# Product-key expert retrieval for 8 samples, laid out by (head, sample) instead of by sample

## The chip, the cores and the metric

The kernel runs on one core of one Trainium2 chip. The metric is the device time of one execution in microseconds; the runs are summed up by their median.

## What is computed

One inference step of a decoder layer for a prompt of 256 tokens and for 8 samples of one token each, D = 2048, all in float32. The change touches the last sublayer, the experts (PEER):

```python
def one(xb):
    q = (xb @ w_pq).reshape(PEER_BLOCK, PEER_HEADS, 2, half)          # 8 heads, 2 x 128
    s1 = jnp.einsum('thd,kd->thk', q[:, :, 0], k1).astype(F32)        # 128 keys
    s2 = jnp.einsum('thd,kd->thk', q[:, :, 1], k2).astype(F32)
    t1, i1 = lax.top_k(s1, PEER_TOPK)                                 # 16 of 128
    t2, i2 = lax.top_k(s2, PEER_TOPK)
    cand = (t1[..., :, None] + t2[..., None, :]).reshape(...)         # 256 candidates
    cidx = (i1[..., :, None] * PEER_KEYS + i2[..., None, :]).reshape(...)
    top, pos = lax.top_k(cand, PEER_TOPK)
    eidx = jnp.take_along_axis(cidx, pos, axis=-1)
    g = jax.nn.softmax(top, axis=-1)
    u = u_tab[eidx]
    v = v_tab[eidx]
    a = jax.nn.gelu(jnp.einsum('thkd,td->thk', u, xb).astype(F32))
    return jnp.einsum('thk,thkd->td', (g * a).astype(v.dtype), v)
```

So each token has 8 heads, each head picks 16 of 16384 experts, and each expert is one row of 2048 numbers (8 KB) in `peer_u` and one in `peer_v`.

## The kernel before

**Blocks.** The 264 tokens are three blocks, `BLOCKS = (P, P, TS)`: two of 128 prompt tokens, one token on a partition, and one of the 8 samples. A token has `SLOTS` = 128 experts (8 heads x 16). Block 0 and block 1 gather their rows slot by slot: one indirect DMA fetches one row of 8 KB for each of 128 partitions. For the samples the 8 x 128 experts are spread over all 128 partitions, so that 8 gathers of u and 8 of v do for all of them; before, partition 16 t + k holds slot k of every head of sample t.

**Order of the expert stage.** The stage runs from about 1340 us to the end. POOL issues all gathers in one order, `pool_gathers` (L1874): first block 0's u rows; then pairs (`pairs`, L1898), of block 1's u row and block 0's v row; then the samples' u and v rows, beside block 1's v rows; then the rest of block 1's v rows. There are 8 slots of 128 x 2048 numbers: 4 for u (even) and 4 for v (odd). Before a u gather POOL waits for a count of dots (`peer_used`), before a v gather for a count of weighted rows (`v_used`). A new index group is copied by two small POOL copies for every four pairs (`indices`, L1892).

**VectorE** forms the dot of each u row with the token's vector (`dve_paired_dots`, L1972, instruction at L1978). Between dots it does the retrieval. For blocks 0 and 1 that goes in 4 parts of 2 heads each; the samples are a part by themselves, number `LAST` = 8, with all 8 heads. A part has three steps, set between loops of dots by hand in the vector program:

```python
            dve_paired_dots(dve, 18, 20)
            dve_keys(dve, LAST)
            dve_paired_dots(dve, 20, 23)
            dve_candidates(dve, LAST)
            dve_paired_dots(dve, 23, 25)
            dve_experts(dve, LAST)
            dve_weights(dve, 1)
            dve_weights(dve, 2)
            dve_paired_dots(dve, 25, 28)
            dve_samples_experts(dve)
```

One loop turn is 4 dots, so `(20, 23)` is 12 dots. A part of block 1 has 8 dots between its steps, and 8 more before the next part's keys. `dve_keys` (L1727) takes the best 16 of 128 scores for each head and key half, `dve_candidates` (L1738) sums them to 256 candidates a head and takes the best 16 of them, both by `dve_sixteen` (L1704: MAX8 at L1715 and L1722, MATCH_REPLACE8 at L1718, FIND_INDEX8 at L1719 and L1725). `dve_experts` (L1758) turns the positions into expert numbers, with six wide operations (L1781, L1784, L1786, twice each). The weights are a softmax: `act_softmax` (L1686) on ScalarE, `dve_weights` (L1794) on VectorE. All operations of VectorE work on rows of a partition, so the samples' ones run on 8 partitions, with 8 heads side by side.

**TensorE** forms the weighted sum of v rows as products with a diagonal matrix of weights (`pe_weighted`, L2004, instruction at L2010); the diagonals come from ScalarE (L1996). The samples' scores are made before the sums begin (`pe_keys(pe, 2)`, L1692, copied out by `act_keys`, L1698). After 26 turns of block 0's sums `pe_samples_experts` (L1826) spreads the samples' expert numbers and weights over the 128 partitions with a selector matrix (`sel`), and `dve_samples_experts` (L1834) masks and reduces them to 8 columns. `sel` also spreads the samples' vectors (`pe_samples_expand`, L1813), and `selT` gathers the partial sums at the end (`pe_samples_sums`, L2066).

Of the kernel before, what the change touches and what calls it, by code (L numbers as in the profile page):

```python
# [23 lines left out]
P = 128  # L24
# [26 lines left out]
for _name, _n in (("ident", P), ("ones", P), ("d0", P), ("d1", TP), ("cb", QB * TP), ("mc", QB * 16), ("ds", PAST + 1),  # L51
                  ("dcs", NC), ("t", TP), ("sel", P), ("selT", TS), ("kmask", 16), ("selk", P), ("kvm", KV), ("iota", 16), ("column", 63), ("pidx", 1),
                  ("half_pi", 1), ("eps", 1)):
    C[_name] = (sum(n for _, n in C.values()), _n)
# [4 lines left out]
def constants():  # L59
    c = np.zeros((P, NCONST), np.float32)  # L60

    def put(name, value):
        a, n = C[name]
        c[: value.shape[0], a:a + n] = value
# [20 lines left out]
    put("sel", (p[None] // 16 == np.arange(TS)[:, None]))  # L85
    put("selT", (p[:, None] // 16 == np.arange(TS)[None]))
    put("kmask", (p[:, None] % 16 == np.arange(16)[None]))
    put("selk", (p[None] % 16 == n[:, None]))
# [41 lines left out]
def build(nc, A):  # L130
    with ExitStack() as ctx:
# [1422 lines left out]

        BLOCKS = (P, P, TS)
        HN = [mv_n[:, 0:D], mv_n[:, D:2 * D], b_st[:, :]]
        XN = [y_t[:, 0:D], y_t[:, D:2 * D], c_st[:, :]]
# [18 lines left out]
        LAST = 2 * PARTS  # L1576
        RETRIEVAL.append((2, 0, PH, LAST * marks(2)[2], x_t[:, D:2 * D], x_t[:, 0:D]))

# [11 lines left out]
        IXS = [z_t[:, 6848 + 8 * i:6856 + 8 * i].bitcast(I32) for i in range(2)]  # L1590
        EXPW = z_t[:, 6880:7008]

# [78 lines left out]
        def act_queries(act):  # L1671
            base = tiles_before["pq"]
            for n in range(16):
                act.wait_ge(S("tile"), base + n + 1)
                act.activation(XQ[:, n, :], bank[n % 4][:, 0:NT], ACT.Copy).then_inc(S("evac"), 1)
                if n >= 4 and n % 4 == 0:
                    act_scores(act, n // 4 - 1)
            act_scores(act, 3)

        def act_scores(act, q):  # L1680
# [5 lines left out]
        def act_softmax(act, blk):  # L1686
            i = (PARTS - 1, LAST - 1, LAST)[blk]
            act.wait_ge(S("tk"), RETRIEVAL[i][3] + marks(RETRIEVAL[i][2] - RETRIEVAL[i][1])[1])
            w = WGT[blk][0:BLOCKS[blk], :]
            act.activation(w, w, ACT.Exp).then_inc(S("tk_exp"), 1)  # L1690

        def pe_keys(pe, blk):  # L1692
            if blk == 2:
                pe.wait_ge(S("sco_act"), PARTS + 4)
            for q in range(4):
                pe_key_scores(pe, blk, q, q)

        def act_keys(act, blk):  # L1698
            n, lo = BLOCKS[blk], (blk - 1) * D
            for q in range(4):  # L1700
                act.wait_ge(S("sco_pe"), 4 * blk + q + 1)
                act.activation(x_t[0:n, lo + q * 512:lo + (q + 1) * 512], bank[q][0:n, :], ACT.Copy).then_inc(S("sco_act"), 1)

        def dve_sixteen(do, n, src, work, groups, width, val, ix):  # L1704
# [22 lines left out]
        def dve_keys(dve, i):  # L1727

            blk, h0, h1, base, sco, _ = RETRIEVAL[i]
            do = Counted(dve, S("tk"), base)  # L1730
            if i:
                do.wait(0)
            dve.wait_ge(S("sco_act"), i + 1 if i < LAST else 4 * (blk + 1))
            c = slice(h0 * 32, h1 * 32)
            dve_sixteen(do, BLOCKS[blk], sco, HOT, 2 * (h1 - h0), PK, VAL[:, c], VIX.bitcast(U32)[:, c])
            assert do.n == marks(h1 - h0)[0]

        def dve_candidates(dve, i):  # L1738

            blk, h0, h1, base, sco, cand = RETRIEVAL[i]  # L1740
            nh = h1 - h0
            n, do = BLOCKS[blk], Counted(dve, S("tk"), base + marks(nh)[0])
            do.wait()
# [14 lines left out]
        def dve_experts(dve, i):  # L1758

            blk, h0, h1, base = RETRIEVAL[i][:4]  # L1760
            nh = h1 - h0
            n, do = BLOCKS[blk], Counted(dve, S("tk"), base + marks(nh)[1])
            do.wait()
# [30 lines left out]
        def dve_weights(dve, blk):  # L1794

            n, do = BLOCKS[blk], Counted(dve, S("wt"), 3 * blk)
            w3 = WGT[blk][0:n, :].rearrange("p (h k) -> p h k", h=PH)
            dve.wait_ge(S("tk_exp"), blk + 1)
            if blk:
                do.wait(0)  # L1800
            do(dve.tensor_reduce(RED[0:n, 0:PH], w3, AXX, ALU.add))
            do.wait()
            do(dve.reciprocal(RED[0:n, PH:2 * PH], RED[0:n, 0:PH]))
            do.wait()
            do(dve.tensor_tensor(w3, w3, RED[0:n, PH:2 * PH].unsqueeze(2).to_broadcast([n, PH, 16]), ALU.mult))

# [6 lines left out]
        def pe_samples_expand(pe):  # L1813
            pe.wait_ge(S("xn"), 6)
            pe.wait_ge(S("sco_act"), PARTS)
            for q in range(4):
                mm = pe.matmul(bank[4 + q][:, :], lhsT=cc("sel", rows=TS), rhs=XN[2][0:TS, q * 512:(q + 1) * 512],
                               start=True, stop=True)
# [7 lines left out]
        def pe_samples_experts(pe):  # L1826
            pe.wait_ge(S("ex_act"), 4)
            pe.wait_ge(S("tk"), RETRIEVAL[LAST][3] + marks(PH)[2] - 1)
            pe.wait_ge(S("wt"), 9)
            pe.matmul(bank[4][:, 0:P], lhsT=cc("sel", rows=TS), rhs=IA[0:TS, :], start=True, stop=True)  # L1830
            pe.matmul(bank[5][:, 0:P], lhsT=cc("sel", rows=TS), rhs=WGT[2][0:TS, :], start=True, stop=True)\
                .then_inc(S("ex_pe"), 1)

        def dve_samples_experts(dve):  # L1834
            do = Counted(dve, S("ex_dve"))
            dve.wait_ge(S("ex_pe"), 2)
            mask = cc("kmask").unsqueeze(1).to_broadcast([P, PH, 16])
            for n, out in enumerate((EXF, WS)):
                if n:
                    do.wait()  # L1840
                do(dve.tensor_tensor(EXPW.rearrange("p (h k) -> p h k", h=PH),
                                     bank[4 + n][:, 0:P].rearrange("p (h k) -> p h k", h=PH), mask, ALU.mult))
                do.wait()
                do(dve.tensor_reduce(out, EXPW.rearrange("p (h k) -> p h k", h=PH), AXX, ALU.add))

            do(dve.tensor_scalar(EXF, EXF, MAGIC, None, ALU.add))
            do.wait()
# [26 lines left out]
        def pool_gathers(pool, use, v_use):  # L1874
# [69 lines left out]

            pool.wait_ge(S("ex_dve"), 7)
            for n, table in enumerate(("peer_u", "peer_v")):
# [71 lines left out]
        def pe_sums0(pe):  # L2018
            pe.wait_ge(S("sco_act"), 12)
            for j in range(4):  # L2020
# [7 lines left out]
        def pe_sums1(pe):  # L2028
            first, last = SLOTS // 4, ALL // 4 - 1
            pe.wait_ge(S("ex_dve"), 7)  # L2030
            for j in range(4):
# [34 lines left out]
        def pe_samples_sums(pe):  # L2066
            pe.wait_ge(S("peer_used"), SUMS_S)
            pe.wait_ge(S("v_out"), 4)
            for q in range(4):
                pe.matmul(bank[q][0:TS, :], lhsT=cc("selT"), rhs=ACC_S[:, q * 512:(q + 1) * 512],  # L2070
                          start=True, stop=True).then_inc(S("sum_pe"), 1)
# [54 lines left out]
        def _(pe):  # L2126
# [4 lines left out]
            pe_samples_expand(pe)  # L2131
            pe_keys(pe, 2)
            pe_sums0(pe)
# [3 lines left out]
        def _(act):  # L2137
# [5 lines left out]
            act_softmax(act, 0)  # L2143
            act_keys(act, 2)
            act_gelu(act, 0)
# [168 lines left out]
```

## Time and profile before

| | |
|---|---|
| median of 3 runs | 2732.05 us (2729.84 to 2735.68) |
| profiled execution, its own time | 2730.46 us |
| its span in the profile | 2728.7 us |
| mean granted TensorE clock | 0.913 |
| busy share PE, DVE, ACT, POOL | 76%, 52%, 11%, 38% |
| moved by the DMAs | 757.94 MB, mean 278 GB/s |

The span is the time from the first to the last instruction that the profiler saw; the execution's own time is 1.8 us longer. PE is TensorE, DVE is VectorE, ACT is ScalarE, POOL is GpSimd. Line numbers (L1978) are those of the kernel. In a timeline a row begins with its start and its duration in us; a bracket at the end gives the idle time of the engine just before it and what ended it. DMA_INDIRECT on POOL is the issue of a gather, not its transfer.

### The profile page before, as it was taken

How to read it: one execution, taken by the hardware profiler on the slowest of the kernel's cores; microseconds unless marked ns; L12 is line 12 of the kernel's file. 1: busy time of each engine (PE TensorE's matmuls, PEld its weight loads, DVE VectorE, ACT ScalarE, POOL GpSimd, SP SyncE). 2: the span in 40 equal slices, each digit the busy share in tenths (PEclk: the TensorE clock that was granted, in tenths of full speed). 3: DMA queues.
4: the chain of work that ended last, by engine and by line, in shares of the span. 5: the costliest groups of instructions: out<-in, count | busy, mean ns of one | idle time of the engine just before them, and what ended most of it. 6: DMA issues, size and time to landing. Idle time of an engine off the chain costs nothing.

```text
span 2728.7 us, 23152 instructions
## 1 busy us (share of the span) xinstructions
PE 2067.7 (76%) x7513; PEld 1292.4 (47%) x7513; DVE 1407.9 (52%) x2520; ACT 290.9 (11%) x733; POOL 1029.7 (38%) x1039
## 2 busy tenths in 40 slices
PE   8999999768889999999960000777777667778776
PEld 6887777545658786288850000222222222223222
DVE  4104565557331105013599999565557674455444
ACT  1001111123210001002010000000000000011000
POOL 2004666362200000000138887555453554445442
PEclk9999999778899999999985555999999889999999
DMA  8434323042234345833679999999999889999997
GB/s 337 144 133 147 109 107 124 36 145 72 77 124 154 141 154 194 315 139 131 263 284 379 427 427 413 427 428 427 428 427 400 363 340 428 427 427 427 428 427 332
DMA packets 107290, 757.94 MB, mean 278 GB/s; under 512 B 12952, under 2 KB 12984, under 8 KB 17800
## 3 DMA queue, kind: packets, MB, share of 16 engines
q0 software_dynamic: 82720, 582.35, 51.6%
q1 hardware_dynamic: 24496, 174.66, 17.7%
q8 instruction: 39, 0.64, 0.1%
q14 instruction: 35, 0.29, 0.0%
HBM read 748.67 MB, written 12.48 MB: 279 GB/s over the span
## 4 chain that ended last, share of the span: by engine, by line
PE 47%; DMA 29%; DVE 13%; issue 7%; POOL 2%; ACT 1%; DVEq 0%; POOLq 0%; SPq 0%; ACTq 0%
PE bank L335 15%; DMA sb_m_t<-in_peer_v,sb_z_t 13%; DMA sb_mk_t<-in_peer_v,sb_z_t 7%; PE bank L2010 6%; PE bank L324 5%; PE bank L670 4%; PE bank L663 4%; DMA sb_mk_t<-in_peer_u,sb_z_t 4%; DVE sb_ring L1969 2%; PE bank L1357 2%; DMA sb_ring<-in_peer_u,sb_z_t 1%; PE bank L1659 1%; DMA sb_ring<-in_peer_v,sb_z_t 1%; PE bank L546 1%; DMA sb_ring<-in_w_z 1%
## 5 line engine op out<-in xcount | busy, mean ns | idle before, releaser
L2010 PE MATMUL bank<-sb_ring,sb_con 128*128 128x512 f32 x800 | 382.5, 624 | 429.2 <-DMA sb_ring<-in_peer_v,sb_z_t 423.9
L2010 PEld LDWEIGHTS bank<-sb_ring,sb_con 128*128 128x128 f32 x800 | 149.6, 196 | 661.2 <-issue 488.2
L1877 POOL DMA_INDIRECT sb_ring<-in_peer_u,sb_z_t x124 | 210.3, 1696 | 132.3 <-DVE sb_ring L1978 44.7
L2010 PE MATMUL bank<-sb_mk_t,sb_con 128*128 128x512 f32 x400 | 186.5, 609 | 58.6 <-DMA sb_mk_t<-in_peer_v,sb_z_t 58.5
L2010 PE MATMUL bank<-sb_m_t,sb_con 128*128 128x512 f32 x400 | 184.6, 604 | 57.8 <-DMA sb_m_t<-in_peer_v,sb_z_t 57.8
L335 PE MATMUL bank<-sb_x_t,sb_ring 128*128 128x264 f32 x1024 | 228.2, 386 | 0.0
L335 PEld LDWEIGHTS bank<-sb_x_t,sb_ring 128*128 128x128 f32 x1024 | 194.6, 190 | 33.2
L1877 POOL DMA_INDIRECT sb_ring<-in_peer_v,sb_z_t x132 | 142.5, 1079 | 179.2 <-PE bank L2010 148.7
L1978 DVE SCALAR_TENSOR_TENSOR sb_ring<-sb_ring,sb_y_t 128x2048 f32<-128x2048 f32 x64 | 146.1, 2291 | 108.1 <-DMA sb_ring<-in_peer_u,sb_z_t 107.4
L335 PE MATMUL bank<-sb_y_t,sb_ring 128*128 128x264 f32 x768 | 171.2, 386 | 0.0
L1996 ACT ACTIVATE sb_con<-sb_con,sb_h_t 128x128 f32<-128x128 f32 x196 | 77.8, 401 | 860.1 <-PE bank L2010 859.4
L1883 POOL COPY sb_z_t<-sb_z_t 128x8 int32<-128x8 int32 x4 | 0.9, 230 | 430.2 <-DVE sb_z_t L1791 426.6
L335 PEld LDWEIGHTS bank<-sb_y_t,sb_ring 128*128 128x128 f32 x768 | 145.9, 190 | 24.9
L2010 PEld LDWEIGHTS bank<-sb_mk_t,sb_con 128*128 128x128 f32 x400 | 72.5, 191 | 172.4 <-issue 83.1
L2010 PEld LDWEIGHTS bank<-sb_m_t,sb_con 128*128 128x128 f32 x400 | 72.0, 189 | 170.1 <-ACT sb_con L1996 83.3
L387 DVE TENSOR_TENSOR sb_h_t<-sb_h_t,bank 128x264 f32 x32 | 13.7, 427 | 232.9 <-PE bank L335 136.1
L1969 DVE SCALAR_TENSOR_TENSOR sb_ring<-sb_ring,sb_y_t 128x2048 f32<-128x2048 f32 x56 | 125.3, 2290 | 0.9 <-DMA sb_ring<-in_peer_u,sb_z_t 0.2
L1877 POOL DMA_INDIRECT sb_m_t<-in_peer_u,sb_z_t x70 | 99.8, 1426 | 55.4 <-DVE sb_m_t L1961 35.9
L663 PE MATMUL bank<-sb_m_t,sb_ring 128*128 128x256 f32 x512 | 116.4, 386 | 3.9 <-DMA sb_ring<-in_w_xk 3.9
L670 PE MATMUL bank<-sb_ring,sb_m_t 128*128 128x256 f32 x512 | 117.9, 389 | 0.0
L1877 POOL DMA_INDIRECT sb_mk_t<-in_peer_v,sb_z_t x66 | 72.8, 1103 | 117.3 <-PE bank L2010 106.1
L1659 PE MATMUL bank<-sb_x_t,sb_ring 128*128 128x264 f32 x512 | 114.6, 386 | 0.0
(431 smaller groups left out, 3231.0 us busy)
## 6 DMA issues: line engine op xcount, KB each, us to landing
sb_ring<-in_w_z SPq DMA_DIRECT2D x28, 1024.0 KB, 4.8
sb_ring<-in_w_xk SPq DMA_DIRECT2D x16, 1024.0 KB, 4.8
sb_ring<-in_w_xv SPq DMA_DIRECT2D x16, 1024.0 KB, 5.1
sb_ring<-in_w_out SPq DMA_DIRECT2D x16, 1024.0 KB, 4.7
sb_ring<-in_w_xq SPq DMA_DIRECT2D x16, 1024.0 KB, 4.8
sb_ring<-in_mem_k SPq DMA_DIRECT2D x16, 1024.0 KB, 4.8
sb_ring<-in_mem_v SPq DMA_DIRECT2D x16, 1024.0 KB, 7.3
sb_ring<-in_w_xo SPq DMA_DIRECT2D x16, 1024.0 KB, 4.8
```

The lines of the kernel that those rows point to most:

```text
L324: mm = pe.matmul(bank[k % 4][:, 0:src.shape[2]], lhsT=R[:, s, t, :], rhs=src[:, t, :], start=(t == 0), stop=(t == kts - 1))
L335: mm = pe.matmul(bank[k][:, 0:src.shape[2]], lhsT=R[:, s, t, :], rhs=src[:, t, :], start=(t == 0), stop=(t == kts - 1))
L546: mm = pe.matmul(bank[4 + part][:, 0:NT], lhsT=BT[32 * jj:32 * jj + 32, part, q, :], rhs=Z[32 * jj:32 * jj + 32, U0 + q, :], start=True, s ...
L663: mm = pe.matmul(bank[n % 4][:, 0:TP], lhsT=R[:, s, t, :], rhs=M[:, t, :], start=(t == 0), stop=(t == KT - 1))
L670: mm = pe.matmul(bank[n % 4][:, 0:TP], lhsT=M[:, t, b * P:(b + 1) * P], rhs=R[:, s:s + 2, t, :], start=(t == 0), stop=(t == KT - 1))
L1357: mm = pe.matmul(bank[3][0:32, :], lhsT=PX[:, m, 32 * r:32 * r + 32], rhs=ring[:, s * D + h * XD:s * D + (h + 1) * XD], start=(j == 0 and ...
L1659: mm = pe.matmul(bank[n % 4][:, 0:NT], lhsT=R[:, s, t, :], rhs=X[:, t, :], start=(t == 0), stop=(t == KT - 1))
L1877: pool.indirect_dma_start(SLOT[slot], None, A[table], bass.IndirectOffsetOnAxis(IXS[half][:, k:k + 1], 0))\
L1969: dve.scalar_tensor_tensor(out=SLOT[k], in0=SLOT[k], scalar=1.0, in1=XN[0], op0=ALU.mult, op1=ALU.mult, accum_out=ACTV[:, bass.ds(i * NSLO ...
L1978: dve.scalar_tensor_tensor(out=SLOT[k], in0=SLOT[k], scalar=1.0, in1=XN[1], op0=ALU.mult, op1=ALU.mult, accum_out=ACTV[:, bass.ds(i * 4 + ...
L1996: act.activation(DIAG[j], ident, ACT.Copy, scale=WGT[blk][:, bass.ds(i * 4 + (j + col), 1)])\
L2010: mm = pe.matmul(bank[b0 + q][:, :], lhsT=DIAG[j], rhs=SLOT[k][:, q * 512:(q + 1) * 512], start=start, stop=stop)
```

## The change

The samples' retrieval is done with one head of one sample on each partition: 64 rows (row h x 8 + t) of 1 head, instead of 8 rows of 8 heads. For that ScalarE copies the samples' queries into the order (half, head, sample) (`QS`), and two products with the 128 keys give the 64 rows of scores. `ROWS` tells the retrieval how many rows a block has. The expert numbers and weights, 16 columns on 64 rows, are brought to 8 columns on 128 partitions by products with the identity, whose second half is put on the upper 64 partitions: partition 64 x half + 8 h + t now holds slots 8 x half to 8 x half + 7 of head h and sample t. The selectors that spread the samples' vectors and collect their sums follow that order (`sel8`, `selT8`, added to the constants beside `sel` and `selT`, 136 columns). How many gathers there are, and where they stand in the order, stays. The diff, cut to its added and removed lines:

```diff
@@ -50,7 +50,7 @@
-                  ("half_pi", 1), ("eps", 1)):
+                  ("half_pi", 1), ("eps", 1), ("sel8", P), ("selT8", TS)):
@@ -84,6 +84,8 @@
+    put("sel8", (p[None] % TS == np.arange(TS)[:, None]))
+    put("selT8", (p[:, None] % TS == np.arange(TS)[None]))
@@ -1553,6 +1555,8 @@
+        ROWS = (P, P, PH * TS)
@@ -1574,7 +1578,7 @@
-        RETRIEVAL.append((2, 0, PH, LAST * marks(2)[2], x_t[:, D:2 * D], x_t[:, 0:D]))
+        RETRIEVAL.append((2, 0, 1, LAST * marks(2)[2], x_t[:, D:D + 256], x_t[:, 0:256]))
         def hw(a, n=SLOTS):
@@ -1588,7 +1592,7 @@
-        EXPW = z_t[:, 6880:7008]
+        QS = z_t[:, 6880:7008]
@@ -1676,6 +1680,8 @@
+            act.activation(QS.rearrange("p (c h t) -> p c h t", c=2, h=PH),
+                           XQ[:, :, TP:NT].rearrange("p (h c) t -> p c h t", c=2), ACT.Copy).then_inc(S("qs"), 1)
         def act_scores(act, q):
@@ -1686,14 +1692,21 @@
         def act_softmax(act, blk):
-            w = WGT[blk][0:BLOCKS[blk], :]
+            w = WGT[blk][0:ROWS[blk], 0:SLOTS if blk < 2 else TOPK]
         def pe_keys(pe, blk):
-            if blk == 2:
-                pe.wait_ge(S("sco_act"), PARTS + 4)
+        def pe_samples_keys(pe):
+            pe.wait_ge(S("sco_act"), PARTS + 4)
+            pe.wait_ge(S("qs"), 1)
+            for c in range(2):
+                mm = pe.matmul(bank[0][0:PH * TS, c * PK:(c + 1) * PK], lhsT=QS[:, c * PH * TS:(c + 1) * PH * TS],
+                               rhs=KEYS[:, c, :], start=True, stop=True)
+            mm.then_inc(S("sco_pe"), 1)
         def act_keys(act, blk):
@@ -1701,6 +1714,10 @@
+        def act_samples_keys(act):
+            act.wait_ge(S("sco_pe"), 9)
+            act.activation(x_t[0:PH * TS, D:D + 256], bank[0][0:PH * TS, 0:256], ACT.Copy).then_inc(S("sco_act"), 1)
         def dve_sixteen(do, n, src, work, groups, width, val, ix):
@@ -1730,16 +1747,16 @@
-            dve.wait_ge(S("sco_act"), i + 1 if i < LAST else 4 * (blk + 1))
+            dve.wait_ge(S("sco_act"), i + 1)
-            dve_sixteen(do, BLOCKS[blk], sco, HOT, 2 * (h1 - h0), PK, VAL[:, c], VIX.bitcast(U32)[:, c])
+            dve_sixteen(do, ROWS[blk], sco, HOT, 2 * (h1 - h0), PK, VAL[:, c], VIX.bitcast(U32)[:, c])
         def dve_candidates(dve, i):
-            n, do = BLOCKS[blk], Counted(dve, S("tk"), base + marks(nh)[0])
+            n, do = ROWS[blk], Counted(dve, S("tk"), base + marks(nh)[0])
@@ -1759,7 +1776,7 @@
-            n, do = BLOCKS[blk], Counted(dve, S("tk"), base + marks(nh)[1])
+            n, do = ROWS[blk], Counted(dve, S("tk"), base + marks(nh)[1])
@@ -1793,16 +1810,16 @@
         def dve_weights(dve, blk):
-            n, do = BLOCKS[blk], Counted(dve, S("wt"), 3 * blk)
-            w3 = WGT[blk][0:n, :].rearrange("p (h k) -> p h k", h=PH)
+            n, do, nh = ROWS[blk], Counted(dve, S("wt"), 3 * blk), PH if blk < 2 else 1
+            w3 = WGT[blk][0:n, 0:nh * TOPK].rearrange("p (h k) -> p h k", h=nh)
-            do(dve.tensor_reduce(RED[0:n, 0:PH], w3, AXX, ALU.add))
-            do.wait()
-            do(dve.reciprocal(RED[0:n, PH:2 * PH], RED[0:n, 0:PH]))
-            do.wait()
-            do(dve.tensor_tensor(w3, w3, RED[0:n, PH:2 * PH].unsqueeze(2).to_broadcast([n, PH, 16]), ALU.mult))
+            do(dve.tensor_reduce(RED[0:n, 0:nh], w3, AXX, ALU.add))
+            do.wait()
+            do(dve.reciprocal(RED[0:n, PH:PH + nh], RED[0:n, 0:nh]))
+            do.wait()
+            do(dve.tensor_tensor(w3, w3, RED[0:n, PH:PH + nh].unsqueeze(2).to_broadcast([n, nh, 16]), ALU.mult))
         def dve_retrieve(dve, i):
@@ -1814,7 +1831,7 @@
-                mm = pe.matmul(bank[4 + q][:, :], lhsT=cc("sel", rows=TS), rhs=XN[2][0:TS, q * 512:(q + 1) * 512],
+                mm = pe.matmul(bank[4 + q][:, :], lhsT=cc("sel8", rows=TS), rhs=XN[2][0:TS, q * 512:(q + 1) * 512],
@@ -1825,25 +1842,20 @@
         def pe_samples_experts(pe):
-            pe.wait_ge(S("tk"), RETRIEVAL[LAST][3] + marks(PH)[2] - 1)
+            pe.wait_ge(S("tk"), RETRIEVAL[LAST][3] + marks(1)[2] - 1)
-            pe.matmul(bank[4][:, 0:P], lhsT=cc("sel", rows=TS), rhs=IA[0:TS, :], start=True, stop=True)
-            pe.matmul(bank[5][:, 0:P], lhsT=cc("sel", rows=TS), rhs=WGT[2][0:TS, :], start=True, stop=True)\
-                .then_inc(S("ex_pe"), 1)
+            for n, src in enumerate((IA, WGT[2])):
+                for half in range(2):
+                    r = slice(64 * half, 64 * half + 64)
+                    mm = pe.matmul(bank[4 + n][r, 0:PH], lhsT=ident[0:64, 0:64], rhs=src[0:64, PH * half:PH * half + PH],
+                                   start=True, stop=True, tile_position=(0, 64 * half))
+            mm.then_inc(S("ex_pe"), 1)
         def dve_samples_experts(dve):
-            mask = cc("kmask").unsqueeze(1).to_broadcast([P, PH, 16])
-            for n, out in enumerate((EXF, WS)):
-                if n:
-                    do.wait()
-                do(dve.tensor_tensor(EXPW.rearrange("p (h k) -> p h k", h=PH),
-                                     bank[4 + n][:, 0:P].rearrange("p (h k) -> p h k", h=PH), mask, ALU.mult))
-                do.wait()
-                do(dve.tensor_reduce(out, EXPW.rearrange("p (h k) -> p h k", h=PH), AXX, ALU.add))
-            do(dve.tensor_scalar(EXF, EXF, MAGIC, None, ALU.add))
+            do(dve.tensor_copy(WS, bank[5][:, 0:PH]))
+            do(dve.tensor_scalar(EXF, bank[4][:, 0:PH], MAGIC, None, ALU.add))
@@ -1942,7 +1954,7 @@
-            pool.wait_ge(S("ex_dve"), 7)
+            pool.wait_ge(S("ex_dve"), 4)
@@ -2016,7 +2028,7 @@
         def pe_sums0(pe):
-            pe.wait_ge(S("sco_act"), 12)
+            pe.wait_ge(S("sco_act"), 9)
@@ -2027,7 +2039,7 @@
         def pe_sums1(pe):
-            pe.wait_ge(S("ex_dve"), 7)
+            pe.wait_ge(S("ex_dve"), 4)
@@ -2067,7 +2079,7 @@
-                pe.matmul(bank[q][0:TS, :], lhsT=cc("selT"), rhs=ACC_S[:, q * 512:(q + 1) * 512],
+                pe.matmul(bank[q][0:TS, :], lhsT=cc("selT8"), rhs=ACC_S[:, q * 512:(q + 1) * 512],
         def dve_samples_out(dve):
@@ -2129,7 +2141,7 @@
-            pe_keys(pe, 2)
+            pe_samples_keys(pe)
@@ -2141,7 +2153,7 @@
-            act_keys(act, 2)
+            act_samples_keys(act)
```

## Rows read from the trace of the kernel before

**Rows 1.** the page, part 4: shares of the chain that ended last, by engine
```profile
PE 47%; DMA 29%; DVE 13%; issue 7%; POOL 2%; ACT 1%; DVEq 0%; POOLq 0%; SPq 0%; ACTq 0%
```

**Rows 2.** windows; columns: us, each engine's busy us (count), PE clock, DMA share, GB/s
```profile
1720.00:2090.00 370.00, 276.57 (x600) 107.48 (x599) 218.36 (x342) 30.12 (x75) 187.29 (x188) 1.00 1.01 427
...
2090.00:2260.00 170.00, 117.30 (x241) 46.41 (x240) 119.18 (x271) 13.44 (x32) 85.80 (x74) 0.90 0.86 355
2110.00:2124.00 14.00, 7.39 (x16) 2.87 (x16) 12.06 (x33) 0.80 (x2) 7.42 (x2) 0.94 0.08 22
2300.00:2700.00 400.00, 305.13 (x655) 118.36 (x654) 198.28 (x115) 39.18 (x91) 185.19 (x201) 0.99 1.01 427
```

**Rows 3.** timeline of POOL; columns: start us, us, engine, line, operation, [idle before, releaser]
```profile
2072.00 0.94 POOL L1877 DMA_INDIRECT sb_m_t<-in_peer_u,sb_z_t  x1 [0.31 <-issue]
...
2116.27 6.62 POOL L1877 DMA_INDIRECT sb_ring<-in_peer_u,sb_z_t  x1 [16.23 <-DVE sb_ring L1978]
...
2186.48 2.18 POOL L1877 DMA_INDIRECT sb_ring<-in_peer_u,sb_z_t  x1 [15.23 <-DVE sb_ring L1978]
...
2232.39 2.18 POOL L1877 DMA_INDIRECT sb_ring<-in_peer_u,sb_z_t  x1 [13.29 <-DVE sb_ring L1978]
```

**Rows 4.** timeline of DVE around the samples' three parts
```profile
2094.08 3.17 DVE L1715 MAX8 sb_h_t<-sb_x_t 8x8 f32<-8x128 f32 x16
...
2113.15 2.26 DVE L1978 SCALAR_TENSOR_TENSOR sb_ring<-sb_ring,sb_y_t 128x2048 f32<-128x2048 f32 x1
...
2165.32 0.28 DVE L1746 CAST sb_h_t<-sb_h_t 8x256 f32<-8x256 uint32 x1
...
2183.00 0.28 DVE L1754 TENSOR_TENSOR sb_h_t<-sb_h_t 8x128 f32<-8x128 f32 x1
2183.32 2.29 DVE L1978 SCALAR_TENSOR_TENSOR sb_ring<-sb_ring,sb_y_t 128x2048 f32<-128x2048 f32 x1
...
2211.82 0.21 DVE L1767 CAST sb_h_t<-sb_h_t 8x128 f32<-8x128 uint32 x1
...
2227.44 0.27 DVE L1801 TENSOR_REDUCE sb_z_t<-sb_h_t 128x8 f32<-128x128 f32 x1
...
2229.23 2.29 DVE L1978 SCALAR_TENSOR_TENSOR sb_ring<-sb_ring,sb_y_t 128x2048 f32<-128x2048 f32 x1
...
2277.54 0.28 DVE L1841 TENSOR_TENSOR sb_z_t<-bank,sb_con 128x128 f32<-128x128 f32 x1
```

**Rows 5.** timeline of DVE around a two-head part of block 1
```profile
1975.51 0.87 DVE L1715 MAX8 sb_h_t<-sb_x_t 128x8 f32<-128x128 f32 x4
...
1980.60 2.27 DVE L1978 SCALAR_TENSOR_TENSOR sb_ring<-sb_ring,sb_y_t 128x2048 f32<-128x2048 f32 x1
...
2014.76 0.19 DVE L1746 CAST sb_h_t<-sb_h_t 128x64 f32<-128x64 uint32 x1
...
2020.12 2.29 DVE L1978 SCALAR_TENSOR_TENSOR sb_ring<-sb_ring,sb_y_t 128x2048 f32<-128x2048 f32 x1
...
2054.85 0.18 DVE L1767 CAST sb_h_t<-sb_h_t 128x32 f32<-128x32 uint32 x1
...
2056.79 0.69 DVE L1784 TENSOR_TENSOR sb_h_t<-sb_h_t 128x512 f32<-128x512 f32 x1
...
2060.96 2.29 DVE L1978 SCALAR_TENSOR_TENSOR sb_ring<-sb_ring,sb_y_t 128x2048 f32<-128x2048 f32 x1
```

**Rows 6.** timeline of ACT in the same stretch
```profile
2193.14 0.51 ACT L1690 ACTIVATE sb_h_t<-sb_h_t 128x128 f32<-128x128 f32 x2
```

**Rows 7.** timeline of PE: the weighted sums and the samples' expert rows
```profile
2231.64 3.69 PE L2010 MATMUL bank<-sb_mk_t,sb_con 128*128 128x512 f32 x8 [1.16 <-DMA sb_mk_t<-in_peer_v,sb_z_t]
2235.26 0.48 PE L1830 MATMUL bank<-sb_h_t,sb_con 8*128 8x128 f32 x2
```

**Rows 8.** timeline of ACT before the samples' vectors are spread
```profile
1404.39 2.07 ACT L1824 ACTIVATE sb_c_st<-bank 128x512 f32<-128x512 f32 x4 [6.54 <-PE bank L1817]
```

**Rows 9.** timeline of PE at the start of the kernel
```profile
11.93 16.69 PE L324 MATMUL bank<-sb_x_t,sb_ring 128*128 128x264 f32 x64 [11.93 <-DMA sb_ring<-in_w_z]
```

## The prediction

> **What bounds the kernel now.** I read the chain first, then windows of the stage that the change touches, then the timelines inside the one window that falls out of line.
>
> The chain's shares by engine [rows 1] say only that TensorE and the DMAs both carry the end: the first 1400 us are matrix products, and the change does not touch them, except that the table of constants grows. What it touches is the expert stage. The windows there [rows 2] are plain. From 1720 to 2090 us and from 2300 to 2700 us the DMA engines are busy all the time (share 1.01) and move 427 GB/s, while TensorE is busy 75% and VectorE 50 to 59% of the time. So the stage is bound by the gathers: one gather is 128 rows of 8 KB, 1.049 MB, and a pair (one u row and one v row for each partition) is 2.097 MB, or 4.91 us at 427 GB/s. Between these stretches lies one that is not bound so: from 2090 to 2260 us only 355 GB/s are moved, and from 2110 to 2124 us next to nothing (share 0.08).
>
> Who holds the gathers up is on POOL's queue [rows 3]. A usual gather is issued after 0.3 us. Three times in this stretch POOL waits 16.23, 15.23 and 13.29 us, each time for VectorE's line 1978, the dot product that frees the next u slot. The v gathers stand behind that wait on the same queue, so both streams dry up. VectorE's timeline [rows 4] shows what it does instead: the retrieval for the 8 samples, in three parts. Keys: 2094.08 to 2113.15, 19.07 us. Candidates: 2165.32 to 2183.32, 18.00 us. Experts, with the weights of block 1 and of the samples: 2211.82 to 2229.23, 17.41 us. 8 partitions carry 8 heads each, so the free dimension is as long as for 128 tokens.
>
> **What the three parts cost in time.** Each part begins right behind a dot product, so their starts serve as marks. Between the starts of keys and candidates lie 12 pairs (dots 20 to 23), between candidates and experts 8 (23 to 25), between experts and the samples' expert list (line 1841, at 2277.54) 12 (25 to 28). The undisturbed pace comes from a part of block 1 [rows 5]: 8 pairs from 1975.51 to 2014.76, 39.25 us, 4.906 each. So:
> keys: 71.24 - 12 x 4.906 = 12.4 us lost;
> candidates: 46.50 - 39.25 = 7.25 us lost;
> experts: 65.72 - 58.87 = 6.85 us lost.
> Together 26.5 us. The windows would say a little more: 170 us x (427 - 355) / 427 = 28.7 us. I take the count of pairs, because the end waits for landed gathers and not for bytes on the way, and keep 28.7 as the upper end. The parts thus hide 6.7 us (19.07 - 12.4) to 10.7 us of their length behind transfers already queued, and show the rest.
>
> **The change part by part.**
> (a) Keys: 16 groups of 128 become 2. A block-1 part has 4 groups on 128 partitions and takes 5.09 us, 1975.51 to 1980.60 [rows 5]; half is 2.55 us. That 64 partitions cost more than 8 is excluded by the same rows: 16 MAX8 on 8 partitions take 3.17 us, 4 on 128 take 0.87, about 0.2 each in both [rows 4, 5].
> (b) Candidates: 8 groups of 256 become 1. The two-head part takes 5.36 us [rows 5]; half is 2.7 us, 2.9 with the small operations that do not halve.
> (c) Experts: six wide operations go from 2048 to 256 elements. At 512 one takes 0.69 us, at 128 0.28 [rows 4, 5]; on the line between them 256 takes 0.42. Six with their gaps are 2.7 us, the six small ones at 0.2 another 1.3: 4.0 us. The two weight steps took 1.79 us, 2227.44 to 2229.23 [rows 4]; block 1's half stays, the samples' shrinks a little: 1.6. Sum 5.6 us.
> VectorE thus loses 54.5 - 11.1 = 43.4 us of work, of which only the 26.5 us that showed can come off the end.
> (d) What is left of the stalls. Three stalls of 2.6, 2.9 and 5.6 us remain. Block 1's part has stalls of 5.09, 5.36 and 6.11 us at the same place of the same loop, and its marks say what they cost: 39.25 us for the 8 pairs after keys, 40.09 after candidates (2014.76 to 2054.85), 39.23 after experts (2054.85 to 2094.08). So a stall of this size costs 0 to 0.85 us. Bounds for three: 0 and 2.6 us; I take 0.4, since two of mine are half as long.
> (e) The samples' list is now made by four products with the identity instead of two with a selector, and four VectorE operations instead of seven. The two old products took 0.48 us for the first and lie between two weighted sums; each of those is 3.69 us in a pair's 4.9, so TensorE has 1.2 us per pair free [rows 7]. If that cover were gone the price is at most about 1 us, because a v slot later by that much is still ahead of three queued gathers. On VectorE the step falls from 1.8 to under 1 us and lies in the free time between dots. Zero.
> (f) The weights wait for the exponentials on ScalarE. These ran at 2193.14 [rows 6], 34 us before their use at 2227.44. Afterwards the use comes about 12 us earlier against the same number of dots (experts 4 us instead of 15.6); the exponentials are released at the end of candidates, 8 dots before, so some 20 us remain. Zero.
> (g) Copy of the queries into another order on ScalarE, once, before the samples' vectors are spread: ScalarE stood idle 6.54 us there [rows 8], one copy of 128 columns is some 0.4 us. Zero. The 16 score products and four copies of the samples become two and one, at a time when TensorE is about to be idle. Zero, nor a gain.
> (h) Constants: 136 more columns, 70 KB, 0.16 us at 427 GB/s, loaded behind the first weight tile. TensorE starts when that tile lands, at 11.93 us, and then runs through [rows 9]. Between 0 and 0.3 us; I take 0.2.
>
> **The sum.** 26.5 - 0.4 - 0.2 = 25.9 us off. The profiled execution took 2730.46 us (span 2728.7), so it would take 2704.6; the median of the runs is 1.6 us above it, hence 2706 us. After 2300 us nothing else takes over: the gathers run at 427 GB/s to the end both in this stretch and in the one before, and TensorE at the full granted clock needs 3.69 us of each 4.91.
>
> A rule against it. Row first: when a stall ends, VectorE runs four ready dots back to back, and POOL's first gather takes 6.62 or 2.18 us instead of 0.94 [rows 3]. The Trainium skill, page "SBUF — State Buffer", in its section on the two sides of SBUF, says that a gather issued by GpSimd needs the port that it shares with VectorE for its descriptors, and that VectorE can lock it out, two-input operations against a GpSimd that reads included. By that rule a short stall also costs issue time, and the time would be that of the first rival below.
>
> **Rivals.**
> A. The issue price stays. Each of the three remaining stalls is followed by slow gathers: 2.18 - 0.94 = 1.2 us for each of two or three, at worst 5.7 us (6.62 - 0.94). Three stalls show 4 to 17 us; 2710 to 2723. For it: the long first gather [rows 3]. Against: after stalls of 5 to 6 us at most 0.85 us was lost. 8%.
> B. The hole is not VectorE's, or the change does not shorten it: 2732 us, no difference. For it nothing but the share that queued transfers hide; against it three waits that name line 1978 and three stalls of their length. 3%.
> C. Slower: without the hole TensorE is clocked down in the long run of sums. At the full granted clock a v row takes 3.69 us; at half, if matmul time doubles, 7.4, which is 2.5 us over the pair's 4.91. The 26.5 us won and the 5.5 for a clear loss are used up by 13 rows at 1.2 GHz, some 95 us; at 20 rows the time is 2732 + 50 - 26 = 2756. It decides from 11 rows on. Against it: 370 us of this same pattern at a granted clock of 1.00 (2.4 GHz) [rows 2]; the dips to 0.90 lie where TensorE starved. 2%.
> D. More than forecast: the window's 28.7 us are all won, 2703.5; within the forecast's range.
> The forecast with D has 87%.
>
> **Range and chances.** Low: 2732 - 28.7 = 2703.4, less 2.4 for the spread that the three runs show below the median; 2701, rounded down to 2700. High: all residues at their upper bounds (2.6 + 0.3 + 1.0), 2732 - 26.5 + 3.9 = 2709.4, plus 3.6 for the spread above, and the lower half of rival A: 2714. A measurement of this kernel tells about 0.2%, 5.5 us, from no change. Faster 0.95 (forecast, D, and A), same 0.03, slower 0.02.
>
> **What would show it.** In the changed kernel: POOL's waits for line 1978 in the samples' parts gone or below 5 us; keys, candidates and experts of the samples at some 2.6, 2.9 and 5.6 us; 12 + 8 + 12 pairs from keys to the samples' list in 157 to 160 us instead of 183.5; the window from 2090 to 2260 us at 420 GB/s or more; everything after it earlier by 26 us, with the same 4.906 us per pair. Wrong if a share below 0.95 remains there, if MAX8 on 64 partitions takes clearly over 0.25 us, if TensorE's v rows take over 4.9 us, or if the stage starts later than now.

## The result and the profile after

| | before | after |
|---|---|---|
| median of 20 runs each | 2734.37 us | 2728.11 us |
| lowest to highest | 2729.84 to 2738.26 | 2724.34 to 2731.49 |
| profiled execution, its span | 2730.46, 2728.7 | 2728.82, 2726.9 |

The ratio is 0.9977 (95% interval 0.9971 to 0.9984): faster by 6.3 us, where 26 were forecast, and outside the range of 2700 to 2714. The sign was right and the size was not. The time of 2728 us is none of the forecast's and its four rivals' either: it lies between the 2710 to 2723 of rival A and the 2732 of rival B.

First the part that the change was made for. These are VectorE's rows at the marks of the samples' three steps (start, duration, engine, line, operation, what it waited for), to be held against [rows 4]:

```profile
2107.15 2.29 DVE L1990 SCALAR_TENSOR_TENSOR sb_mk_t<-sb_mk_t,sb_y_t 128x2048 f32<-128x2048 f32 x1 [2.68 <-DMA sb_mk_t<-in_peer_u,sb_z_t]
...
2109.37 0.47 DVE L1732 MAX8 sb_h_t<-sb_x_t 64x8 f32<-64x128 f32 x2
...
2112.13 2.29 DVE L1990 SCALAR_TENSOR_TENSOR sb_ring<-sb_ring,sb_y_t 128x2048 f32<-128x2048 f32 x1
...
2169.11 0.17 DVE L1763 CAST sb_h_t<-sb_h_t 64x32 f32<-64x32 uint32 x1
...
2172.31 2.29 DVE L1990 SCALAR_TENSOR_TENSOR sb_ring<-sb_ring,sb_y_t 128x2048 f32<-128x2048 f32 x1 [0.15 <-issue]
...
2208.92 0.16 DVE L1784 CAST sb_h_t<-sb_h_t 64x16 f32<-64x16 uint32 x1
...
2210.49 0.42 DVE L1801 TENSOR_TENSOR sb_h_t<-sb_h_t 64x256 f32<-64x256 f32 x1
...
2214.53 2.29 DVE L1990 SCALAR_TENSOR_TENSOR sb_ring<-sb_ring,sb_y_t 128x2048 f32<-128x2048 f32 x1 [0.17 <-issue]
...
2269.65 0.16 DVE L1857 COPY sb_z_t<-bank 128x8 f32<-128x8 f32 x1
```

Keys now take 2.76 us (2109.37 to 2112.13), candidates 3.20, experts with the weights 5.61; 19.07, 18.00 and 17.41 before. POOL's rows in the same stretch, against [rows 3]:

```profile
2110.55 0.93 POOL L1889 DMA_INDIRECT sb_mk_t<-in_peer_u,sb_z_t  x1 [0.31 <-issue]
2114.11 1.12 POOL L1889 DMA_INDIRECT sb_mk_t<-in_peer_v,sb_z_t  x1 [2.63 <-PE bank L2022]
...
2213.68 0.95 POOL L1889 DMA_INDIRECT sb_mk_t<-in_peer_v,sb_z_t  x1 [2.41 <-PE bank L2022]
2214.64 2.22 POOL L1906 COPY sb_z_t<-sb_z_t 128x4 int32 x1
2216.81 2.26 POOL L1907 COPY sb_z_t<-sb_z_t 128x4 int32 x1
2219.87 0.96 POOL L1889 DMA_INDIRECT sb_ring<-in_peer_u,sb_z_t  x1 [0.80 <-POOL sb_z_t L1907]
```

No gather waits for the dot product any more; the waits of 16.23, 15.23 and 13.29 us are gone. So the hole is closed. The windows of the stage, however, against [rows 2] (the last three columns are TensorE's granted clock, the DMA share and GB/s):

```profile
1720.00:2090.00 370.00, 274.81 (x593) 107.03 (x592) 216.10 (x340) 29.72 (x74) 187.34 (x186) 1.00 1.01 421
2090.00:2260.00 170.00, 125.71 (x281) 48.93 (x279) 88.17 (x113) 15.35 (x37) 79.30 (x87) 1.00 1.01 421
2300.00:2700.00 400.00, 299.74 (x648) 116.22 (x647) 194.39 (x112) 38.38 (x89) 183.65 (x197) 1.00 1.01 421
```

The chain's shares by engine [rows 1] say of this only that VectorE's part fell (13 to 10%) and the DMAs' rose (29 to 32%):

```profile
PE 49%; DMA 32%; DVE 10%; issue 6%; POOL 3%; ACT 1%; POOLq 0%; DVEq 0%; SPq 0%; ACTq 0%
```

In the windows, the middle row went from 355 to 421 GB/s, as it should. But the rows above and below it, where the change does nothing, went from 427 to 421, with the DMA engines as busy as before (1.01) and TensorE's granted clock at 1.00. The transfers themselves became slower, for the whole stage. Nor is it TensorE: from 1460 to 1690 us, where only block 0's u rows are gathered and TensorE does nothing, the rate fell as well. Before:

```profile
1460.00:1690.00 230.00, 0.00 (x0) 0.00 (x0) 227.53 (x258) 0.00 (x0) 190.49 (x106) 0.50 1.01 426
```

After:

```profile
1460.00:1690.00 230.00, 0.00 (x0) 0.00 (x0) 225.70 (x256) 0.00 (x0) 190.25 (x105) 0.50 1.01 420
```

To see it per pair, take POOL's last gather and the 56th before it, 28 pairs apart. In the kernel before:

```profile
2560.85 1.23 POOL L1877 DMA_INDIRECT sb_mk_t<-in_peer_v,sb_z_t  x1 [2.41 <-PE bank L2010]
...
2698.22 1.23 POOL L1877 DMA_INDIRECT sb_mk_t<-in_peer_v,sb_z_t  x1 [2.41 <-PE bank L2010]
```

The same two rows in the kernel after:

```profile
2556.86 1.28 POOL L1889 DMA_INDIRECT sb_mk_t<-in_peer_v,sb_z_t  x1 [2.47 <-PE bank L2022]
...
2696.14 1.28 POOL L1889 DMA_INDIRECT sb_mk_t<-in_peer_v,sb_z_t  x1 [2.46 <-PE bank L2022]
```

137.37 / 28 = 4.906 us per pair before, 139.28 / 28 = 4.974 after. Below, "pace" is always this number. The stage has 528 gathers; from the 129th on they come in pairs, 200 of them, and 200 x 0.068 is 13.6 us.

Why should the same gathers be slower? One thing that the change moves without a line of the diff saying so: `con`, the table of constants, is the first tile allocated in SBUF, and 136 more columns of 4 bytes move every tile behind it by 544 bytes. The 8 slots that the gathers write are `ring` (4), `mk_t` (2) and `m_t` (2). Their start addresses within a partition, modulo 256 bytes, were 0, 0 and 96 and are now 32, 32 and 128. The tiles between them move too, among them `y_t` (the tokens' vectors) and `z_t` (which holds the gathers' indices).

### The profile page after: what moved, and what is told of

Same layout as the page of the kernel before. It is cut to its first block, busy times and chain, and to the rows that moved or that the text cites. A ratio compares the mean times of both kernels' runs of the same rounds, so it can differ in the third digit from the quotient of the medians.

```text
span 2726.9 us, 22932 instructions
## 1 busy us (share of the span) xinstructions
PE 2056.5 (75%) x7489; PEld 1287.5 (47%) x7489; DVE 1364.7 (50%) x2349; ACT 289.4 (11%) x731; POOL 1018.9 (37%) x1039
## 4 chain that ended last, share of the span: by engine, by line
PE 49%; DMA 32%; DVE 10%; issue 6%; POOL 3%; ACT 1%; POOLq 0%; DVEq 0%; SPq 0%; ACTq 0%
PE bank L337 15%; DMA sb_mk_t<-in_peer_v,sb_z_t 15%; DMA sb_m_t<-in_peer_v,sb_z_t 12%; PE bank L2022 6%; PE bank L326 6%; PE bank L672 4%; PE bank L665 4%; DMA sb_mk_t<-in_peer_u,sb_z_t 3%; PE bank L1359 2%; DVE sb_ring L1981 2%; DMA sb_ring<-in_peer_u,sb_z_t 1%; PE bank L1663 1%; POOL sb_ring L1889 1%; PE bank L548 1%; PE bank L613 1%
## 5 line engine op out<-in xcount | busy, mean ns | idle before, releaser
L2022 PE MATMUL bank<-sb_ring,sb_con 128*128 128x512 f32 x800 | 374.8, 612 | 426.3 <-DMA sb_ring<-in_peer_v,sb_z_t 421.1
L1889 POOL DMA_INDIRECT sb_ring<-in_peer_u,sb_z_t x124 | 199.5, 1609 | 89.8 <-issue 25.4
L337 PE MATMUL bank<-sb_x_t,sb_ring 128*128 128x264 f32 x1024 | 228.2, 386 | 0.0
L1889 POOL DMA_INDIRECT sb_m_t<-in_peer_v,sb_z_t x66 | 71.7, 1086 | 123.2 <-PE bank L2022 112.5
```

Source lines behind the costliest of these rows:

```text
L337: mm = pe.matmul(bank[k][:, 0:src.shape[2]], lhsT=R[:, s, t, :], rhs=src[:, t, :], start=(t == 0), stop=(t == kts - 1))
L1889: pool.indirect_dma_start(SLOT[slot], None, A[table], bass.IndirectOffsetOnAxis(IXS[half][:, k:k + 1], 0))\
L2022: mm = pe.matmul(bank[b0 + q][:, :], lhsT=DIAG[j], rhs=SLOT[k][:, q * 512:(q + 1) * 512], start=start, stop=stop)
```

## The experiments

Three theories went in (their letters are not those of the prediction's rivals). **A**: where on the chip the gathered rows are written sets the rate. **B**: the wider constants lay out the inputs in HBM in another way, and reading is slower. **C**: without the holes the queues are fuller, and fuller queues run slower. The first three kernels tell them apart, and the fourth asks for the best version. All pads are tiles that nothing uses.

**The kernel before, its addresses moved as the change moves them:**

```diff
         con = sb("con", NCONST)
+        sb("pad0", 136)
         gain = sb("gain", NGAIN)
```

> The kernel before, with 136 unused columns (544 bytes per partition) laid behind the constants on chip: every later tensor, the eight gather slots among them, then stands at the address it has in the changed kernel. No instruction and no transfer changes. Theory A (the start address of the slots on chip sets the gathers' rate): 4.98 us per pair instead of 4.906, from about 1340 us to the end, some 1.45% of 1290 us: 17 to 20 us slower, about 2752 us, ratio 1.006 to 1.007. Theory B (the place or size of the tensors in HBM) and theory C (the changed retrieval itself, by its fuller queues, slows the gathers): ratio 1.000, 4.906 us per pair.

2749.19 us (2746.62 to 2751.84), ratio 1.0054 (1.0041 to 1.0068), that is 16.4 us over the 2732.76 us of before, measured beside it, and a little less than the 17 to 20 expected. One unused tile, nothing else. Its last gathers, and its windows:

```profile
2579.76 1.29 POOL L1878 DMA_INDIRECT sb_mk_t<-in_peer_v,sb_z_t  x1 [2.45 <-PE bank L2011]
...
2719.23 1.29 POOL L1878 DMA_INDIRECT sb_mk_t<-in_peer_v,sb_z_t  x1 [2.47 <-PE bank L2011]
```

```profile
1720.00:2090.00 370.00, 273.42 (x594) 106.31 (x593) 216.22 (x340) 29.71 (x74) 187.96 (x187) 1.00 1.01 421
2090.00:2260.00 170.00, 114.79 (x238) 45.37 (x237) 119.93 (x272) 13.43 (x32) 79.98 (x70) 0.91 0.88 357
2300.00:2700.00 400.00, 299.10 (x644) 115.84 (x643) 195.54 (x117) 38.79 (x90) 183.41 (x197) 0.99 1.01 421
```

The pace is 4.981 at 421 GB/s, and the hole (share 0.88) is still there. The slower transfers have nothing to do with the retrieval, and C falls.

**The kernel after, its addresses put back** (544 + 480 = 1024 bytes, so every tile stands modulo 1024 as before):

```diff
         con = sb("con", NCONST)
+        sb("pad0", 120)
```

> The changed kernel with 120 more unused columns (480 bytes) behind the constants, so that the sum of the shift is 1024 bytes and each slot stands, counted modulo 512, where it stood before. Theory A: 4.906 us per pair again, the three stalls gone, so the 26 us of the prediction come back: 2704 to 2710 us, ratio 0.990 to 0.992. Theories B and C: 4.977 us per pair and 2728 us as the changed kernel, ratio 0.998.

2710.59 us (2710.1 to 2711.75), ratio 0.9916 (0.9903 to 0.9930), pace 4.905: pace and ratio as theory A expected. Its first two windows (the third reaches past its last gather):

```profile
1720.00:2090.00 370.00, 278.90 (x601) 108.72 (x600) 219.53 (x343) 30.52 (x76) 189.68 (x190) 1.00 1.01 427
2090.00:2260.00 170.00, 127.97 (x285) 50.32 (x286) 89.03 (x119) 15.36 (x37) 79.99 (x86) 1.00 1.01 427
```

**The kernel before with the wider constants in HBM alone** (`consts` has 136 more columns there, and the load takes `[:, 0:NCONST]`; the line that fills the wider table is left out here):

```diff
-    "consts": (P, NCONST), ...
+    "consts": (P, NCONST + 136), ...
-        sp.dma_start(con[:, :], A["consts"])
+        sp.dma_start(con[:, :], A["consts"][:, 0:NCONST])
```

> The kernel before, with the input of constants 136 columns wider in HBM but only the old 2078 columns loaded; the tables behind it in HBM move by the same 70 KB as in the changed kernel, the layout on chip stays. Theory B: 4.98 us per pair, ratio 1.006 to 1.007. Theories A and C: no change, ratio within 0.999 to 1.001.

2734.27 us, ratio 1.0003 (0.9994 to 1.0012), pace 4.906: no difference, and B falls.

**The kernel after with all 8 slots on a 256-byte boundary:**

```diff
+        sb("pad0", 120)
         gain = sb("gain", NGAIN)
+        sb("pad1", 104)
         m_t = sb("m_t", KT * TP)
+        sb("pad2", 24)
         ring = sb("ring", 4 * D)
```

> The changed kernel with pads (120, 104 and 24 columns) so that all eight gather slots start at a multiple of 512 bytes; before, six did and the two in the tile m_t stood 96 bytes past one. Theory A, if each slot off the boundary costs by itself: going from 6 of 8 slots aligned to 0 cost 1.45%, so the last two should give about a third of that, 0.4 to 0.5%: 4.88 us per pair and 5 to 7 us less than the kernel shifted by 1024, 2699 to 2703 us. Theories B and C: 2728 us.

2708.78 us (2707.27 to 2711.45), ratio 0.9911 (0.9895 to 0.9926). It is the lowest median of all and beats both kernels, but it lies only 1.8 us below the second experiment where 5 to 7 were expected, which these few runs do not even tell apart. Its pace is the same 4.906, although the issue of a v gather takes 1.27 to 1.28 us here as in the kernel after, so the issue is not what made the pairs slower:

```profile
2538.97 1.27 POOL L1892 DMA_INDIRECT sb_mk_t<-in_peer_v,sb_z_t  x1 [2.42 <-PE bank L2025]
...
2676.34 1.28 POOL L1892 DMA_INDIRECT sb_mk_t<-in_peer_v,sb_z_t  x1 [2.42 <-PE bank L2025]
```

That was a miss: the two slots of `m_t`, 96 bytes off in the kernel before, cost nothing there. So either 96 bytes is harmless, or two slots of eight are. It shows one thing more: `y_t` and `z_t` also stood 96 bytes off in the kernel before and stand on the boundary here, and the pace is the same.

**How far off matters?** From that kernel, `pad0` alone grows, and all 8 slots, with every other tile behind the constants, move together by 32, 64, 96, 128 and 256 bytes (`pad0` of 128, 136, 144, 152 and 184). The first of them:

```diff
-        sb("pad0", 120)
+        sb("pad0", 128)
```

> The changed kernel with all eight gather slots 32 bytes past a multiple of 512. Read by the pace of the last 28 pairs (4.906 us with all slots on the boundary, 4.974 in the changed kernel with six at 32 and two at 128). Theory A1 (each row costs the bytes from the last 256-byte boundary again, 32 of 8192): 4.925 us. Theory A2 (only a start off a multiple of 64 costs, a fixed price): 6 of 8 slots cost 0.068 us, so 8 of 8 cost 0.091: 4.997 us. Theory A3 (any start off 512 costs the same): 0.068 for 8 slots, 4.974 us.

> All slots 64 bytes past a multiple of 512. A1: 4.944 us per pair. A2: 4.906 us. A3: 4.974 us.

> All slots 96 bytes past a multiple of 512. A1: 4.963 us per pair. A2: 4.997 us, the same as at 32. A3: 4.974 us. A fourth reading, that 96 is free, would fit the kernel before, whose two slots at 96 cost nothing against the kernel with all eight on the boundary: 4.906 us.

> All slots 128 bytes past a multiple of 512. A1: 4.983 us per pair. A2: 4.906 us. A3: 4.974 us.

> The changed kernel with all eight slots 256 bytes past a multiple of 512. At 32, 64, 96 and 128 bytes a pair took 4.970 to 4.988 us, on the boundary 4.906. If the boundary that counts is 256 bytes: 4.906 us. If it is 512: 4.97 us.

| all 8 slots past the boundary by | pace, us | time, us | ratio to before (95%) |
|---|---|---|---|
| 0 bytes | 4.906 | 2708.78 | 0.9911 (0.9895 to 0.9926) |
| 32 | 4.988 | 2730.70 | 0.9980 (0.9968 to 0.9991) |
| 64 | 4.970 | 2723.50 | 0.9958 (0.9939 to 0.9978) |
| 96 | 4.969 | 2725.77 | 0.9978 (0.9965 to 0.9990) |
| 128 | 4.974 | 2725.14 | 0.9962 (0.9949 to 0.9976) |
| 256 | 4.906 | 2709.17 (one run) | |

The row of 0 bytes is the fourth experiment. Not all times were measured side by side; the ratios, each to runs of before beside it, compare better.

The cost is there or not, and hardly depends on the distance: 1.3 to 1.4% of the pace from 64 to 128 bytes, 1.7% at 32. A cost in proportion to the distance (A1) falls, and so does a boundary at 64 bytes (A2); A3, one price at any distance, comes nearest. How far can a pace be trusted? All kernels with at most two slots off lie within 0.001 us of each other (4.905 to 4.906), but the kernel after and the first experiment, whose slots stand at the same addresses, gave 4.974 and 4.981. So the three paces from 4.969 to 4.974 are alike. That 32 bytes costs more is seen in the time too: 2730.70 us against 2723.50 to 2725.77 for the other three, measured side by side. 96 bytes is not harmless, so it must be the number of slots.

**How many slots?** From the same kernel, `ring` alone moved by 64 bytes (4 of 8):

```diff
-        sb("pad2", 24)
+        sb("pad2", 40)
         ring = sb("ring", 4 * D)
+        sb("pad3", 112)
         mk_t = sb("mk_t", KT * TP)
```

then `ring` and `m_t` (6 of 8), where `pad2` stays at 24 (`y_t`, `z_t` and `gate`, which lie between the two, move by 64 bytes with them):

```diff
-        sb("pad1", 104)
+        sb("pad1", 120)
         m_t = sb("m_t", KT * TP)
...
+        sb("pad3", 112)
         mk_t = sb("mk_t", KT * TP)
```

> Only the four slots of the ring 64 bytes off, the four of m_t and mk_t on the boundary. The kernel before has 2 of 8 slots off and its pairs take 4.906 us, as with all 8 on: a quarter cost nothing. Theory M (two limits side by side: 4.906 us from one of them, which does not depend on the start, and the writes on chip, 4.97 us a pair off the boundary and some 4.82 to 4.88 on it, of which the mean over the slots counts): with half of them off 4.906 to 4.93 us. Theory L (each slot costs its share, and the quarter of the kernel before is free for another reason, such as the tile m_t): 4.938 us with 4 of 8.

> The ring's four slots and the two of m_t 64 bytes off, mk_t on the boundary: 6 of 8. Theory M: 4.93 to 4.95 us per pair (for 4.82 us on the boundary 0.75 x 4.97 + 0.25 x 4.82 = 4.93). Theory L with a share each: 4.954 us; if m_t is free by nature: 4.938, as with the ring alone.

The pace is 4.916 with four slots off and 4.944 with six, inside the ranges of theory M and 0.022 and 0.010 below the figures of theory L; another 28 pairs of the same profiles, 108 gathers further up, give 4.916 and 4.943. The times are 2716.20 and 2716.69 us in one run each. The pace is told apart by these runs, the times, with one run each, are not. With 4.970 for eight slots (64 bytes), each further quarter of the slots costs 0.027 us: 4.916, 4.944, 4.970. The same line gives 4.889 for two slots and 4.862 for none, both under 4.906. An account that fits all of them is a floor of 4.906 us that something else sets, and a cost of writing that shows only once its mean over the eight slots is above this floor. The floor was measured (0 and 2 of 8 slots off both give it); the line below it is an extrapolation.

Of these kernels only the one with `ring` moved changes the address of the slots and of nothing else (the tiles behind the ring move by 512 bytes there, which leaves them where they were modulo 256). That the slots' addresses count is shown by it, with 0.010 us. That the rest of the 0.068 us is theirs as well is argued: by the even steps from four to eight slots, and by `y_t` and `z_t`, which cost nothing at 96 bytes.

**Does the length of VectorE's stall count, or the kind of work?** In the kernel of the second experiment, 24 memsets of 128x512, each waited for, were put ahead of the samples' keys, to bring back one long stall with other work in it:

```diff
+            for n in range(24):
+                dve.memset(idle[:, 0:512], 0.0).then_inc(S("idle"), 1)
+                dve.wait_ge(S("idle"), n + 1)
             dve_keys(dve, LAST)
```

> The changed kernel at the old addresses modulo 512, with 24 writes of 512 unused columns (0.5 us each) before the samples' keys, so that this step holds VectorE about 15 us instead of 2.75. By the prediction's account a stall hides 6.7 to 10.7 us behind queued gathers and shows the rest: 4.5 to 8.5 us lost between the starts of keys and candidates against 12 pairs at 4.906, and the samples' other two steps lose nothing. A rival, that what hides depends on the length of the stall alone and all beyond 6.1 us shows: 9 us. If the three stalls cost nothing but by something else in the old retrieval (the 8-partition operations): 0.

One run, 2717.24 us. VectorE's rows at the marks, and POOL's first gather behind the stall:

```profile
2092.43 2.29 DVE L1992 SCALAR_TENSOR_TENSOR sb_mk_t<-sb_mk_t,sb_y_t 128x2048 f32<-128x2048 f32 x1 [2.59 <-DMA sb_mk_t<-in_peer_u,sb_z_t]
...
2094.78 0.48 DVE L2208 MEMSET sb_idle<- 128x512 f32 x1
...
2113.18 2.26 DVE L1992 SCALAR_TENSOR_TENSOR sb_ring<-sb_ring,sb_y_t 128x2048 f32<-128x2048 f32 x1
...
2165.45 0.17 DVE L1765 CAST sb_h_t<-sb_h_t 64x32 f32<-64x32 uint32 x1
```

```profile
2116.30 6.62 POOL L1891 DMA_INDIRECT sb_ring<-in_peer_u,sb_z_t  x1 [15.71 <-DVE sb_ring L1992]
```

A memset with its wait took 0.66 us, so the stall came out at 18.5 us (2094.65 to 2113.18), longer than meant. From its start to the candidates lie 12 pairs in 70.80 us; 70.80 - 58.87 = 11.9 us lost, and 6.6 hidden. Before, a stall of 19.07 us lost 12.4 and hid 6.7 [rows 4]. From the 129th gather to the last this kernel took 990.4 us, about 12 more than the second experiment (978.2). So at this place of the loop the length counts, and not the kind of work. What is hidden is another matter: the expected 4.5 to 8.5 us were for a stall of 15 us; for 18.5 us the same account gives 7.8 to 11.8, and the rival, which lets all beyond 6.1 us show, 12.4. 11.9 lies between the two, and this one run does not decide. Nor does length alone set the loss at every place: the candidates' stall of 18.00 us lost only 7.25. Even the first gather behind the stall takes the same 6.62 us as in [rows 3].

## Why the prediction was right in one half and wrong in the other

**The failed step is (h), the constants.** It priced the 136 columns as "70 KB, 0.16 us at 427 GB/s" and stopped there: it counted their transfer and not the room that they take in front of everything else. With it fell the last sentence of the sum, that after 2300 us the gathers run "at 427 GB/s to the end", and the same pace of 4.906 us in the list of what would show it. Instead of 0.2 us the term cost 16.4 (before with and without the 544 bytes) or 17.5 (2728.11 - 2710.59, after with and without them; by their ratios to before, since they were not measured side by side, 16.7). The second can be followed in the two profiles: from the 129th gather to the last, after took 993.1 us and the second experiment 978.2, 14.9 more, of which 200 pairs at 4.974 instead of 4.905 are 13.8. Of the u gathers ahead of them the 57th to the 113th came every 2.499 us instead of 2.473, and the 129th was issued 3.0 us later. No row of before named the addresses. But the trace showed that the stage hangs on the rate of one kind of transfer from about 1460 us to the end, and then everything that can touch that rate had to be named. 1% of it is 12 us, half the forecast.

**The retrieval was priced right.** With the addresses put back, the change gives 2732.76 - 2710.59 = 22.2 us (by the interval 19 to 26.5) against 25.9 forecast. In the profiles, from the issue of the 129th gather to that of the last, before took 1005.2 us (1693.1 to 2698.2), the third experiment 1003.7, and the second 978.2: 25.4 to 26.9 us less. The medians' 22.2 is a little smaller; the interval holds both. What lies ahead of the 129th gather differs by more than that between two profiles of the same instructions (it was issued at 1693.1 us in before and at 1699.4 in the third experiment), so whether the change costs anything there is open. The two effects add up: 22.2 - 16.4 = 5.8 us, and 6.3 were measured.
- (a) keys 2.76 us against 2.55 to 2.6, (b) candidates 3.20 against 2.7 to 2.9, (c) experts and weights 5.61 against 5.6. MAX8 on 64 partitions takes 0.235 us.
- (d) what the remaining stalls lose: in the kernel after 59.74, 39.81 and 60.73 us for 12, 8 and 12 pairs, at 4.974 each 0.0, 0.0 and 1.0 us; in the second experiment 0.0, 0.0 and 0.9. Forecast 0.4, with bounds of 0 and 2.6. The forecast took its pace of 4.906 from 8 pairs behind a stall of 5.09 us, where a loss would have been hidden in the pace; the last 28 pairs, without such a stall, give the same 4.906.
- (e), (f), (g) nothing, as forecast: the list's four products and two copies lie beside dots, the samples' exponentials (the second row) end over 18 us before their use at 2213.76, and ScalarE's copy of the queries fits in its idle time. The rows of after:

```profile
1402.84 0.30 ACT L1683 ACTIVATE sb_z_t<-sb_z_t 128x128 f32<-128x128 f32 x1
...
2194.82 0.41 ACT L1696 ACTIVATE sb_h_t<-sb_h_t 128x128 f32<-128x128 f32 x2
...
2213.76 0.16 DVE L1818 TENSOR_REDUCE sb_z_t<-sb_h_t 64x1 f32<-64x16 f32 x1
```

**The rivals.** A, the issue price: the rows show it (two copies on POOL of 2.2 us instead of 0.19, behind the experts), but it is within the 1.0 us above. The Trainium skill, page "SBUF — State Buffer", in its section on the two sides of SBUF, says that a VectorE instruction with two inputs in SBUF and a GpSimd instruction that reads SBUF block each other on the port that they share. In direction the trace agrees: these copies, and the gather of 6.62 us, ran beside dots back to back. After stalls of up to 5.6 us that has no price of its own in the time. B, no hole: false. C, TensorE clocked down: false, the granted clock is 1.00 in all three windows. D, 28.7 us: the pairs' count (26.5) was the better of the two, as far as 25.4 to 26.9 can tell.

## What to carry to other kernels

Where a stage is bound by transfers, the start addresses of their destination tiles can be part of its price: a constant that grows by a few hundred bytes moves every tile allocated behind it. When a change allocates or widens anything, work out which tiles move, and put those that large gathers write on 256-byte boundaries. And when a forecast gain does not arrive, compare first the stretches that the change does not touch: here they told at once that the loss was not in the retrieval.

## What the runs showed of the hardware

A stream of gathers of 128 rows of 8 KB, one for each partition, was slower when the starts of its destinations were off a 256-byte boundary in the partition, and the share of such slots decided how much: nothing with two slots of eight (96 bytes off), 0.2% with four and 0.8% with six (64 bytes off), 1.3 to 1.7% with eight. With all eight together 0 and 256 bytes were fast and 32, 64, 96 and 128 slow; distances from 160 to 224 were not tried. The Trainium skill, page "DMA: Bandwidth & Descriptors", in its section on how a descriptor splits into AXI transactions, says that a descriptor which does not start on a multiple of 256 bytes begins its first transaction at the boundary below, and that the bytes ahead of its start are fetched but unused and still cost beats, of 32 bytes each. That speaks of the side that is read, and here it was the side that is written that moved. The boundary agrees. The size does not: by an estimate from that rule 32 bytes would cost least and 128 four times as much, and here 32 cost most (4.988) and the other three were alike (4.969 to 4.974). Why the cost is flat, and what sets the floor of 4.906 us, no run here shows.
